# Scores of two MLA heads made together at the end of every second slot, in a hybrid decoder trunk

## The reference

```
def causal_block_scores(q_blk, k_ctx, q_start, scale, slopes=None):
    s = jnp.einsum('bhqd,bhkd->bhqk', q_blk, k_ctx).astype(jnp.float32) * scale
    ...
    return jnp.where(dist >= 0, s, -jnp.inf)

def mla_attention(q, k, v):
    S = q.shape[2]
    scale = (MLA_NOPE + MLA_ROPE) ** -0.5
    outs = []
    for i in range(S // Q_BLOCK):
        start, end = i * Q_BLOCK, (i + 1) * Q_BLOCK
        p = jax.nn.softmax(causal_block_scores(q[:, :, start:end], k[:, :, :end], start, scale), axis=-1)
        outs.append(jnp.einsum('bhqk,bhkd->bhqd', p.astype(v.dtype), v[:, :, :end]))
    return jnp.concatenate(outs, axis=2)
    ...
    q = jnp.concatenate([q[..., :MLA_NOPE], apply_rope(q[..., MLA_NOPE:], pos)], axis=-1)
    ...
    k = jnp.concatenate([kv[..., :MLA_NOPE], jnp.broadcast_to(k_rope, (B, MLA_HEADS, S, MLA_ROPE))], axis=-1)
```

## Time and profile before

| | us |
|---|---|
| median of 3 runs | 1291.36 |
| lowest, highest | 1285.52, 1291.74 |
| the profiled execution's own time | 1292.49 |
| its span | 1290.4 |
| PE busy | 1246.0 (97%) |
| DVE busy | 1000.5 (78%) |
| ACT busy | 820.2 (64%) |

### The profile page before, as it was taken

The page is one execution under the profiler, slowest core; times in us unless marked ns, Lnnn a source line. Parts: engine busy times, 40 slices in busy tenths (PEclk is TensorE's granted clock), DMA queues, the critical chain, the costliest instruction groups (busy, mean ns, idle before and its releaser), DMA issues.

```text
span 1290.4 us, 17437 instructions
## 1 busy us (share of the span) xinstructions
PE 1246.0 (97%) x6182; PEld 1035.3 (80%) x6182; DVE 1000.5 (78%) x1165; ACT 820.2 (64%) x912; POOL 46.9 (4%) x57
## 2 busy tenths in 40 slices
PE   6989899999899998999999999999999999999997
PEld 6876688888798676888888888888888888888885
DVE  5764656565666647889989989989989989989986
ACT  6265454455534745777777777777777777777774
POOL 2000000000000001000000000000000000000000
PEclk9999899999999897999999999999999999999999
DMA  9320665555334039999999999999999999999961
GB/s 304 106 98 1 203 218 180 189 184 178 118 111 155 25 101 397 367 364 374 353 362 376 352 360 376 351 362 375 350 362 374 353 362 375 351 364 372 352 234 49
DMA packets 184738, 349.63 MB, mean 271 GB/s; under 512 B 15063, under 2 KB 72981, under 8 KB 184692
## 3 DMA queue, kind: packets, MB, share of 16 engines
q1 hardware_dynamic: 182428, 341.22, 74.8%
q0 software_dynamic: 2064, 7.27, 1.6%
q10 hardware_dynamic: 200, 0.54, 0.1%
HBM read 346.91 MB, written 2.10 MB: 270 GB/s over the span
## 4 chain that ended last, share of the span: by engine, by line
PE 93%; ACT 2%; DVE 2%; DMA 1%; issue 1%; SPq 0%; POOL 0%; POOLq 0%; DVEq 0%
PE bank L1499 23%; PE bank L1501 22%; PE bank L1500 22%; PE bank L1775 6%; PE bank L1776 3%; PE bank L1556 3%; PE bank L1567 2%; PE bank L1841 1%; PE bank L1591 1%; PE bank L1660 1%; DMA raw_a<-in_w_gate_dense 1%; PE bank L1588 1%; PE bank L1509 1%; PE bank L1807 1%; PE bank L1822 1%
## 5 line engine op out<-in xcount | busy, mean ns | idle before, releaser
L1032 DVE TENSOR_TENSOR lo_ring<-raw_m,hi_ring 128x2048 fp32r<-128x2048 f32 x168 | 382.9, 2287 | 51.7 <-ACT hi_ring L701 51.6
L701 ACT ACTIVATE hi_ring<-raw_m 128x2048 fp32r<-128x2048 f32 x168 | 322.2, 1919 | 83.9 <-PE bank L1501 83.9
L1499 PE MATMUL bank<-hi_ring,hT 128*128 128x512 f32 (+1 forms) x832 | 318.6, 383 | 0.0
L1501 PE MATMUL bank<-hi_ring,hT 128*128 128x512 f32 (+1 forms) x832 | 312.3, 375 | 0.0
L1500 PE MATMUL bank<-lo_ring,hT 128*128 128x512 f32 (+1 forms) x832 | 311.8, 375 | 0.0
L1032 DVE TENSOR_TENSOR lo_ring<-raw_a,hi_ring 128x2048 fp32r<-128x2048 f32 x96 | 219.0, 2290 | 32.2 <-ACT hi_ring L701 32.2
L701 ACT ACTIVATE hi_ring<-raw_a 128x2048 fp32r<-128x2048 f32 x96 | 183.5, 1919 | 53.9 <-PE bank L1501 53.9
L1499 PEld LDWEIGHTS bank<-hi_ring,hT 128*128 128x128 f32 x832 | 157.7, 190 | 28.9 <-DVE lo_ring L1032 2.4
L1501 PEld LDWEIGHTS bank<-hi_ring,hT 128*128 128x128 f32 x832 | 157.3, 189 | 28.4
L1500 PEld LDWEIGHTS bank<-lo_ring,hT 128*128 128x128 f32 x832 | 157.7, 190 | 26.4
L1027 DVE TENSOR_TENSOR lo_ring<-raw_a,hi_ring 128x2048 fp32r<-128x2048 f32 (+1 forms) x49 | 110.5, 2259 | 69.0 <-ACT hi_ring L695 69.0
(11 more groups left out here) (293 smaller groups left out, 1448.9 us busy)
## 6 DMA issues: line engine op xcount, KB each, us to landing
raw_m<-in_w_down_exp SPq DMA_DIRECT2D x80, 1024.0 KB, 5.6
raw_a<-in_w_up_exp SPq DMA_DIRECT2D x48, 1024.0 KB, 5.7
raw_m<-in_w_gate_exp SPq DMA_DIRECT2D x48, 1024.0 KB, 5.8
raw_a<-in_w_gate_exp SPq DMA_DIRECT2D x40, 1024.0 KB, 5.5
raw_m<-in_w_up_exp SPq DMA_DIRECT2D x40, 1024.0 KB, 6.1
raw_a<-in_w_in SPq DMA_DIRECT2D x12, 1024.0 KB, 7.1
raw_a<-in_w_gate_dense SPq DMA_DIRECT2D x11, 1024.0 KB, 5.4
raw_a<-in_w_up_dense SPq DMA_DIRECT2D x11, 1024.0 KB, 5.4
```

The source lines that it names most:

```text
L701: A(hi_of(NA + j), t, ACT.Copy).then_inc(hi_ready, 1)
L1032: V.tensor_tensor(lo_of(NA + j), expert_slot(i, j)[0], hi_of(NA + j).bitcast(F32), ALU.subtract).then_inc(lo_ready, 1)
L1499: M(o, lh, rh, start=start, stop=False)
L1501: return M(o, ll, rh, start=False, stop=stop)
```

## The change

scores keeps the differential heads. A new function, scores_pair, makes the scores of two MLA heads: content of both heads for the first block, content of both for the second, then rope of both for the first and rope of both for the second, each time alternating between the two heads, whose operands lie in two row groups and whose results lie in two banks. It first waits for both banks. Only the first product into each bank has start=True. Scores of slots 6 and 7 are made at the end of iteration 4, those of 8 and 9 at the end of iteration 6, those of 10 and 11 at the end of iteration 8, each time behind the transposes. The numbers of products and their sizes are the same; DVE, ACT and SP have the same instructions in the same order.

```diff
--- before.py
+++ after.py
@@ -1568,30 +1568,42 @@
                                       start=k == 0, stop=k == KT - 1)
                     r.then_inc(piece_used, 1)
 
+                def free_scores(u):
+                    if u >= 3:
+                        pe.wait_ge(s_max, 2 * (UNITS * l + u - 2))
+
                 def scores(k):
+                    h, _ = head_of(k)
                     for u in units_of(k):
                         if u == 0:
                             pe.wait_ge(proj_evac, NIN * l + 7)
                         if u == 2:
                             pe.wait_ge(proj_evac, NIN * (l + 1))
-                        if u >= 3:
-                            pe.wait_ge(s_max, 2 * (UNITS * l + u - 2))
-                        h, _ = head_of(k)
-                        if k < HEADS:
-                            r0 = (h % 2) * DV + (u % 2) * HD
-                            q, kk = dqk[r0:r0 + HD, h // 2, :], dqk[r0:r0 + HD, 3 + h // 2, :]
-                        else:
-                            r0, g0 = (h % 2) * NOPE, (h % 3) * ROPE
-                            q, kk = q_nope[r0:r0 + NOPE, h // 2, :], k_nope[r0:r0 + NOPE, h // 2, :]
-                            qr, kkr = q_rope[g0:g0 + ROPE, h // 3, :], kr[g0:g0 + ROPE, :]
+                        free_scores(u)
+                        r0 = (h % 2) * DV + (u % 2) * HD
+                        q, kk = dqk[r0:r0 + HD, h // 2, :], dqk[r0:r0 + HD, 3 + h // 2, :]
                         b = bank[S_BANK[u % 3]]
-                        M(b[:, 0:P], q[:, 0:P], kk[:, 0:P], start=True, stop=k < HEADS)
-                        if k >= HEADS:
-                            M(b[:, 0:P], qr[:, 0:P], kkr[:, 0:P], start=False, stop=True)
-                        r = M(b[:, P:3 * P], q[:, P:2 * P], kk[:, :], start=True, stop=k < HEADS)
-                        if k >= HEADS:
-                            r = M(b[:, P:3 * P], qr[:, P:2 * P], kkr[:, :], start=False, stop=True)
-                        r.then_inc(s_mm, 1)
+                        M(b[:, 0:P], q[:, 0:P], kk[:, 0:P], start=True, stop=True)
+                        M(b[:, P:3 * P], q[:, P:2 * P], kk[:, :], start=True, stop=True).then_inc(s_mm, 1)
+
+                def scores_pair(k):
+
+                    heads = []
+                    for m in (k, k + 1):
+                        u, (h, _) = units_of(m)[0], head_of(m)
+                        free_scores(u)
+                        r0, g0 = (h % 2) * NOPE, (h % 3) * ROPE
+                        heads.append((bank[S_BANK[u % 3]],
+                                      q_nope[r0:r0 + NOPE, h // 2, :], k_nope[r0:r0 + NOPE, h // 2, :],
+                                      q_rope[g0:g0 + ROPE, h // 3, :], kr[g0:g0 + ROPE, :]))
+                    for b, q, kk, _, _ in heads:
+                        M(b[:, 0:P], q[:, 0:P], kk[:, 0:P], start=True, stop=False)
+                    for b, q, kk, _, _ in heads:
+                        M(b[:, P:3 * P], q[:, P:2 * P], kk, start=False, stop=False)
+                    for b, _, _, qr, kkr in heads:
+                        M(b[:, 0:P], qr[:, 0:P], kkr[:, 0:P], start=False, stop=False)
+                    for b, _, _, qr, kkr in heads:
+                        M(b[:, P:3 * P], qr[:, P:2 * P], kkr, start=False, stop=True).then_inc(s_mm, 1)
 
                 for p in range(NIN):
                     project(p)
@@ -1708,7 +1720,7 @@
 
                 scores(1)
                 for k in range(SLOTS + 1):
-                    if k + 2 < SLOTS:
+                    if k + 2 < HEADS:
                         scores(k + 2)
                     if k == SLOTS:
                         pe.wait_ge(conv_step, CS * (l + 1))
@@ -1728,6 +1740,8 @@
                         values(k - 1)
                     if k < SLOTS:
                         transposes(k)
+                    if k % 2 == 0 and HEADS <= k + 2 < SLOTS:
+                        scores_pair(k + 2)
                     if k == 2:
                         pe.wait_ge(conv_step, CS * l + CS_TAPS)
                         for c in range(2):
```

## The result

| | before | changed |
|---|---|---|
| median, us | 1289.07 (4 runs) | 1308.70 (4 runs) |
| lowest, highest | 1285.52, 1291.74 | 1306.72, 1310.35 |
| ratio to before, 95% interval | | 1.0148 [1.0123, 1.0173] |
| profiled execution: its time, its span | 1292.49, 1290.4 | 1307.24, 1305.2 |

The changed kernel is 19.6 us slower. In a second set of runs (e6) its median lies 19.8 us above that of before. The ratio with its interval is one figure for both sets, not two independent ones.

A forecast was written before the change was run, and what follows sets the result against it. PE, busy 18.09 of 18.10 us, was taken to set the pace of the MLA slots. Walks +8.8, output quarter -1.0 and clock +5.2 gave +13.0 on 1291.36, so 1304.4 us; range 1296 to 1313.

The forecast's parts named there:

- PE's saving: MLA scores: a pair costs 1.72 us instead of 4.16, saving 14.6 us of PE work over 3 pairs and 2 layers.
- PE's busy time about 10 us lower: Sign expected in the profile after: PE's busy time falls by about 10 us while the span is longer.
- The three walks: Transposes of slots 4 to 6, 6 to 8, 8 to 10: 7.70, 9.26, 8.30 us; 8.8 us added over both layers.
- The steps named: Signs in the MLA slots: PE idle before L1738 (squares on ACT) and before the values of slots 7, 8 and 9.
- The clock: PE's new waits in the MLA slots halve the clock for one PE part of a walk per layer: +5.2 us.
- layer 0's output quarter: First quarter of output projection, behind slot 10's transposes: halved clock may not recur, so 1.0 us comes off.
- rival 1: MLA slots: same walks but the clock stays full, 1299.2 us; chance 20%.
- Rival 2: Clock half from slot 4 to 10 in both layers, 1320.6 us; chance 8%.
- No overlap: MLA pairs: products of 64 rows do not overlap, a pair costs 3.04 us, 1312.3 us in all; chance 7%.
- PE as the bound: Iterations 4 to 9: PE remains the bound, so 14.6 us come off, 1276.8 us; chance 8%.

The follow-up runs named there:

- e6: The changed kernel run again without an edit, in a second set: 1308.52 us against 1288.70 for before, ratio 1.0148.
- e3: Changed kernel plus fillers (products whose result nobody reads) in PE's waits behind the pairs and later transposes: 1300.96 us against 1290.42 for before, ratio 1.0086.
- e1: Changed kernel with each pair moved to the beginning of its iteration, the old place of scores: 1288.86 us against 1290.42 for before, ratio 0.9990.
- e2: Kernel before with unpaired single heads, moved to the late place behind the transposes: 1317.50 us against 1290.42 for before, ratio 1.0221.
- e4: Kernel before with each head's products grouped, both content then both rope, single heads at the old place: 1287.91 us against 1290.42, ratio 0.9981.
- e8: Changed kernel with pairs at the beginning of iterations, plus unused products in PE's waits: 1282.49 us against 1288.70 for before, ratio 0.9942.
- e7: Kernel before with grouped content and rope, plus unused products in differential slots and behind slot 9: 1283.28 us against 1288.70 for before, ratio 0.9952.
- e9: Kernel before, scores untouched, plus unused products in differential slots and behind slot 9: 1286.68 us against 1289.13 for before, ratio 0.9976.

## Why the prediction was right, and what it mis-sized

The forecast was +13.0 us and 1304.4. The median came to 1308.70, inside the range of 1296 to 1313 but 4.3 above the forecast, and the difference to before was 19.6. The forecast stood on a median of 1291.36, before's later one is 1289.07; part of the closeness of the totals is this accident.

**PE's saving.** 1.72 us per pair was right (446.54 to the filler at 448.25 in e3, 1.71 us), and so was the overlap of products of 64 rows in different row groups. Nothing of it was left: the waits took all. The sign "PE's busy time about 10 us lower" did not come, it was 3.5 us: the products of slowed stretches last longer.

**The three walks.** 25.26 us were worked out and 25.05 measured at full clock (e3), each of the three within 0.12. The steps named are those at which PE waits in the trace: L1738 for ACT's squares, the values of slots 7, 8 and 9 for ACT's copies. e1 shows that the place makes them as long as they are: with the same pairs ahead of the values PE waits at the same lines, but 0.8 to 1.6 us at a time and not up to 2.5. e2 shows that without pairing the place is worse.

**The clock.** This term was mis-sized. I charged 5.2 us, one PE part of a walk per layer; in the first profile each layer had two slowed stretches. The walks took 56.4 us in the first profile and 58.3 in the second, against 50.1 in e3: 6.3 and 8.2 us. And I took 1.0 off for layer 0's output quarter, reading its halved clock before as a thing that need not recur. It recurred in both layers: from slot 10 to 11 it took 7.81 and 7.56 us, against 6.44 and 6.48 at full clock, so the term was +1.4 over before and not -1.0. Walks at full clock 8.4, clock in them 6.3, output quarter 1.4, less 0.8 in the differential slots (30.1 against 30.9 us): 15.3 us, beside 14.8 between the two spans. The rest up to 19.6, 4.9 us, is in the choice of executions: before's profiled one (1292.49) took 3.4 us longer than its median, the changed one's (1307.24) 1.5 less than its own. By "the clock stays full" (rival 1) it would have been 7.8 us above before; e3, which has the full clock in the MLA slots, lies 10.5 above in medians and 7.7 in spans. Rival 2, half throughout, did not come true either, though the third walk of layer 0 ran whole at 0.50.

What a PE with more waits loses was right in direction for this change: 0.75 and 0.85 with PE busy for two thirds of the stage, 1.00 with the fillers. As a rule it did not hold from run to run. In e2 PE was busy for 11.97 us of a walk of 12.55 and had 0.50, in the changed kernel for 4.65 of 9.18 and had 1.00. In the kernel before too, over 420.30 to 435.00, the clock was 0.59 with PE busy for 14.41 of 14.70 us; the prediction counts that place as agreement, but the busy share there does not say so. The place of the Trainium skill that was weighed there ("TensorE: Matmul & The Clock Gate", "What's actually happening": the ratio follows how busy PE has been) agrees with the trace in the comparison of the changed kernel with e3, and a walk's busy share alone does not give its clock in e2. No run here shows what decides where in a stage the clock falls.

**The rivals that fell.** No overlap: the pair took 1.7 us. PE as the bound: with early pairs (e1) PE waits for ACT in every slot from 6 on. That one contained a piece of truth, though: before, PE was the bound, and with 0.38 us less per head (e4) the stage became 1.6 us shorter. It then meets the loop through DVE and ACT at about 18.9 us, whether PE's scores are pairs (e1, e8) or grouped heads (e4, e7). Neither engine is full there: in e8 DVE is busy for 13.05 and ACT for 14.63 of 18.90 us. It is the order of their steps that takes the time.

## What to carry to other kernels

An engine that is busy throughout a stage can be relieved, but the relief is worth only the distance to the next limit, and the position of the relieved work in the engine's order may be worth more: a product that feeds a loop through three in-order engines belongs ahead of the waits of that loop, however much cheaper it becomes in a group behind them. Such a loop can be walked from the starts in a timeline, here to 0.12 us per walk at the full clock. Where a change makes TensorE wait, a halved clock is a cost of its own, here 6.3 and 8.2 us in two profiles of one kernel, and products without a use in the waits brought it back (e3).

## What the runs showed of the hardware that was not expected

- A change between products of 64 and of 32 rows cost 0.19 us: content, rope, content, rope took 2.08 us per head, content, content, rope, rope 1.70 (e4), with the same products and two changes fewer. The change that is left in e4, from the wide content to the narrow rope product, has the same size: 0.52 us from the wide product's start (104.93 to 105.45) and 0.33 from the narrow one's, against 0.43 and 0.22 for a wide and a narrow product of one height (443.53, 443.96 and 444.18 in e1). The wide content and the narrow rope product write different columns, so the cost does not come from adding to columns just written. Overlap of two heads in different row groups brought two heads to 1.72.
- In a differential head's scores the two units start together although the first unit's wide product stands between them in program order. The trace shows it by lines: four records of L1588 before the first of L1591 against an order of L1588, L1591, L1588, L1591. So with products of one height the alternation need not be written out by hand. With mixed heights neighbouring row groups are not enough: in e2 the second head of a pair, in the other row group, starts at 459.88, when the first is through (457.80 to 459.88), and the two take 4.17 us. Two grouped heads right behind each other were not run, so whether grouping alone would give the pair's 1.72 us stays open.
- Fillers shortened a kernel: 14 products more (17493 instructions in e9 against 17437) and 2.5 us less.
